# Four stage borders of a hybrid decoder step on one Trainium2 core: a head norm reordered, new queries built earlier, value rows written by panel, two mixture tiles and one third of a panel done before a border

## The chip, the core and the metric

The kernel runs on one core of a Trainium2 chip. The metric is the device time of one execution in microseconds. Engines are called by the names of the profile: PE (TensorE, with PEld for its weight loads), DVE (VectorE), ACT (ScalarE), POOL (GpSimd) and SP (SyncE, whose queue issues nearly every DMA here).

## What is computed

One inference step of a two-layer decoder trunk, for a prompt of 1024 tokens and 8 samples of 4 new tokens each (1056 token columns in all). Cut to what matters:

```
for l in range(2):
    h = rmsnorm(x, g_norm1[l]) * (1 + sc1) + sh1            # sh, sc, g come from c @ w_ada
    q_a, k_a, v_a, i, f, o, u, q_c, k_c, v_c, f_c = split(h @ w_in[l] + b_in[l])
    ha = sigmoid(o) * headnorm(mlstm(q_a, k_a, v_a, i, f))   # chunks of 128, 4 heads
    hb = pool_mix(u)                                         # windows 2, 4, 8, 16
    hc = forgetting_attention(q_c, k_c, v_c, f_c)            # 6 heads of 64; samples read 16 pages of cache each
    x = x + g1 * (concat(ha, hb, hc) @ w_out[l])
    h2 = rmsnorm(x, g_norm2[l]) * (1 + sc2) + sh2
    x = x + g2 * (relu(h2 @ w_up[l])**2 @ w_down[l])
y = rmsnorm(x, g_final)
```

Keys, values, forget values and the recurrent states of both layers are outputs too.

## The kernel before

Everything is feature major: 128 features on the partitions, 1056 token columns along the free axis. Large products are done in two-part fp32r: an operand is a high part (a cast) and a low part (operand minus high part), and each product is three matmuls, high x high, low x high and high x low. The 1056 columns are cut in three *parts* of 352 (`CW`), so one panel of 128 output features is three *thirds* of 24 matmuls each (`part_product`, L307; in the projection `third`, L851). Weights come in panels of 128 x 1024: SP loads one into `raw`, POOL casts it to `whi` (L295), DVE subtracts to `wlo` (L300).

A layer is three blocks of code, and between two blocks all engines meet at a barrier; between the layers there are two barriers, since one more block clears semaphores. All orders are written out by hand, per engine, with semaphore waits.

- **`projection(l)`**: 21 panels (rows of `F`, in the order `PANEL_ROWS`). From panel 9 on, chunk `u` of the mLSTM is interleaved with the thirds of panel `n = START + u`; chunk 8 (`CH`) is the samples. DVE works through `square_heads(u-1)`, `clip(u)`, `keys(u)` (L1281, L1288), `scale_query(u)` (L1299 to L1306), `norm_heads(u-1)` (L1365 to L1367), `weigh(u)`, `join(u-1)`. PE turns the normed heads with `turn_heads` (L967), which waits for `norm_heads`. The last thing on PE is `turn_values` (L979), which turns the value rows into `vC`. In layer 1 the block begins with panels 0 and 1 part by part, because the norm of the last 352 columns is unfinished: `sums` (L593), a third of panel 0 with `spread` (L604) inside it, and so on.
- **`attention(l)`**: 24 units (3 pairs of heads x 8 query blocks) of the prompt, with the 8 samples interleaved, one per three units: `scores(b)` (L1712) needs 16 pages of the cache, four per *step*, and `past_mixed(b)` (L1748) uses them. Pages lie in a ring of 24 buffers `KVp`, six steps. SP's program there is serial: pages of the first sample, three rows of past sums (L1567), 8 page numbers (each a register load), 8 pages, 16 page numbers, and then per step a wait for the ring and four pages. The start of the block also has GpSimd's `row_spread` (L1596), masks, `Qb` (the new queries of the samples, laid out in blocks, L1610); PE's `forget` (L1646), whose results DVE and ACT copy into `Fb` (L1831, L1965). `Fb` overwrites value rows of `F`, so these copies wait until the value rows are stored in `o_v` (L782).
- **`out_and_mlp(l)`**: the output projection by phases: thirds (panel, part) in the order (0,0), (1,0), (0,1), (1,1), (2,0), (2,1), ... Its operand is the mixture, eight tiles of `F` (`MIX`), cast to `hH` (ACT L2257 for part 0, POOL L2100 for parts 1 and 2) and reduced to `hL` by DVE (L2300). `x` was spilled and is reloaded (L2073). Then the MLP, and at its end, again by phases, residual and norm for the next layer.

PE's third waits read, for instance, as

```
def turn_heads(u):
    pe.wait_ge(S["normal"], u + 1)
...
by_phases(0, (hH, hL), lambda part, k: pe.wait_ge(mixed, KT * part + k + 1))
```

## Time and profile before

| | |
|---|---|
| runs shown | 2780.46, 2784.61, 2788.09 us (median 2784.61) |
| profiled execution, its own time | 2787.31 us |
| its span | 2785.5 us |
| PE busy | 2691.4 us (97%) |
| DVE, ACT, POOL busy | 1238.0, 633.8, 264.4 us |
| mean granted clock | 0.988 |
| projection of layer 0, attention, output projection and MLP | about 54 to 381 us, 381 to 557, 557 to 1431 |
| the same of layer 1 | 1431 to 1750, 1750 to 1928, 1928 to 2785 |

The profile is one execution recorded by the hardware. PE is busy nearly throughout, so what matters is the short list of places where it is not: the view of waits gives, per engine and line, who was waited for, in total, how often, and the longest. A timeline shows start, duration, engine, line, operation, and in square brackets the idle time just before with its releaser; matmuls overlap, so durations of single matmuls are longer than their distance. The view by windows gives busy times of a stretch and the granted clock of PE, where 1.00 is 2.4 GHz and 0.50 is 1.2 GHz.

### The profile page before, as it was taken

Reading aid. Unit: us, or ns where it says so; the run is one execution under the profiler, and the core shown is the slowest. Engines: PE = TensorE matmul, PEld = TensorE weight load, DVE = VectorE, ACT = ScalarE, POOL = GpSimd, SP = SyncE. Lnnn points to the kernel's source line nnn. Section 1 sums busy time; section 2 is a strip of 40 time slices with the busy share of each in tenths; the row PEclk is TensorE's granted clock in tenths of the full one; section 3 lists DMA queues with packets and bytes.
Section 4 is the critical chain, followed back from the end, with each engine's and each line's share of the span. In section 5 each row is a group of like instructions: output and inputs, shape, how many; then the busy total and the mean of one; then the engine's idle time right before and its main releaser. Section 6 shows DMA issues by size and latency. Waiting matters only on the chain. (4 is left out here: it accounts for less than half of the span.)

```text
span 2785.5 us, 48553 instructions
## 1 busy us (share of the span) xinstructions
PE 2691.4 (97%) x20596; PEld 2511.2 (90%) x20596; DVE 1238.0 (44%) x2223; ACT 633.8 (23%) x1044; POOL 264.4 (9%) x342
## 2 busy tenths in 40 slices
PE   5999989999999999999999999898999999999998
PEld 4999966699999999999989999566999999999998
DVE  5735535647423423324457354456563242242344
ACT  4334334423110110001133432343221000000012
POOL 0101100020000000001111010001100000000010
PEclk9999999999999999999999999999999999999999
DMA  8440168631222221111133102885212111111111
GB/s 308 155 109 31 67 243 319 246 116 46 84 84 91 76 91 61 54 46 46 61 112 118 52 31 88 316 324 197 81 54 71 46 45 53 46 54 46 46 55 69
DMA packets 106873, 295.37 MB, mean 106 GB/s; under 512 B 19605, under 2 KB 32790, under 8 KB 104610
## 3 DMA queue, kind: packets, MB, share of 16 engines
q1 hardware_dynamic: 106498, 291.49, 30.3%
q8 instruction: 163, 2.67, 0.4%
q0 software_dynamic: 160, 0.79, 0.1%
q14 instruction: 52, 0.43, 0.0%
HBM read 269.61 MB, written 22.63 MB: 105 GB/s over the span
## 5 line engine op out<-in xcount | busy, mean ns | idle before, releaser
L307 PE MATMUL PS<-hH,whi 128*128 128x352 f32 x1632 | 534.3, 327 | 8.0 <-DVE hL L2300 6.4
L307 PE MATMUL PS<-hL,whi 128*128 128x352 f32 x1632 | 525.4, 322 | 0.0
L307 PE MATMUL PS<-hH,wlo 128*128 128x352 f32 x1632 | 524.9, 322 | 0.0
L307 PE MATMUL PS<-aH,whi 128*128 128x352 f32 x1344 | 439.4, 327 | 4.0 <-PEq L384 3.2
L307 PE MATMUL PS<-aL,whi 128*128 128x352 f32 x1344 | 432.2, 322 | 0.0
L307 PE MATMUL PS<-aH,wlo 128*128 128x352 f32 x1344 | 431.9, 321 | 0.0
L295 POOL CAST whi<-raw 128x1024 fp32r<-128x1024 f32 x158 | 166.5, 1054 | 1673.2 <-PE PS L307 1332.6
L307 PEld LDWEIGHTS PS<-hH,whi 128*128 128x128 f32 x1632 | 307.8, 189 | 16.1 <-issue 12.7
L307 PEld LDWEIGHTS PS<-hL,whi 128*128 128x128 f32 x1632 | 308.5, 189 | 0.0
L307 PEld LDWEIGHTS PS<-hH,wlo 128*128 128x128 f32 x1632 | 307.8, 189 | 0.0
L851 PE MATMUL PS<-aH,whi 128*128 128x352 f32 x912 | 303.6, 333 | 1.9 <-ACT F L1060 1.9
L851 PE MATMUL PS<-aH,wlo 128*128 128x352 f32 x912 | 293.6, 322 | 0.0
L851 PE MATMUL PS<-aL,whi 128*128 128x352 f32 x912 | 293.2, 322 | 0.0
L307 PEld LDWEIGHTS PS<-aH,whi 128*128 128x128 f32 x1344 | 253.5, 189 | 9.5 <-issue 4.7
L307 PEld LDWEIGHTS PS<-aL,whi 128*128 128x128 f32 x1344 | 253.9, 189 | 0.0
L307 PEld LDWEIGHTS PS<-aH,wlo 128*128 128x128 f32 x1344 | 253.1, 188 | 0.0
L300 DVE TENSOR_TENSOR wlo<-raw,whi 128x1024 fp32r<-128x1024 f32 x160 | 195.8, 1223 | 126.3 <-POOL whi L295 124.6
L2384 DVE TENSOR_TENSOR aH<-ev 128x1056 fp32r<-128x1056 f32 x64 | 84.0, 1313 | 272.1 <-ACT ev L2269 272.1
L2269 ACT ACTIVATE ev<-PS 128x1056 f32<-128x1056 f32 x64 | 67.6, 1056 | 573.2 <-PE PS L307 573.2
L851 PEld LDWEIGHTS PS<-aH,whi 128*128 128x128 f32 x912 | 171.7, 188 | 10.5 <-issue 4.2
L851 PEld LDWEIGHTS PS<-aL,whi 128*128 128x128 f32 x912 | 172.2, 189 | 0.4
L851 PEld LDWEIGHTS PS<-aH,wlo 128*128 128x128 f32 x912 | 171.9, 189 | 0.0
(367 smaller groups left out, 3563.2 us busy)
## 6 DMA issues: line engine op xcount, KB each, us to landing
KVp<-kv SPq DMA_DIRECT2D x256, 384.0 KB, 7.3
raw<-w_ff SPq DMA_DIRECT2D x128, 512.0 KB, 3.6
raw<-w_in SPq DMA_DIRECT2D x42, 512.0 KB, 3.5
wad_single<-w_ada SPq DMA_DIRECT2D x40, 512.0 KB, 3.6
wad<-w_ada SPq DMA_DIRECT2D x32, 512.0 KB, 5.6
x_spill<-x SPq DMA_DIRECT2D x2, 4224.0 KB, 13.3
wada<-w_first SPq DMA_DIRECT2D x8, 1024.0 KB, 7.0
raw<-w_out SPq DMA_DIRECT2D x16, 512.0 KB, 4.1
```

The source lines that it names most:

```text
L295: nc.gpsimd.tensor_copy(home(n)[0][:], raw[spot(n)][:]).then_inc(s["high"], 1)
L300: nc.vector.tensor_tensor(wl[:], raw[spot(n)][:], wh[:].bitcast(F32), ALU.subtract).then_inc(s["split"], 1)
L307: last = nc.tensor.matmul(PS[:, 3 * p + part, 0:CW], w[:, k, :], a[:, k, part * CW:(part + 1) * CW], start=k == 0 and w is wh and a is hig ...
L851: last = nc.tensor.matmul(PS[:, part, 0:CW], w[:, k, :], a[:, k, part * CW:(part + 1) * CW], start=k == 0 and w is whi[n % 2] and a is aH, ...
L2269: nc.scalar.activation(three(ev[n % 2][:]), banks(n % 2), ACT.Relu).then_inc(s["room"], NCH)
L2384: link(nc.vector.tensor_tensor(aH[:, j, :], t, t, ALU.mult))
```

## The change

It edits five places.

1. **Projection, unit 8.** DVE does `norm_heads(7)` ahead of `keys(8)` and `scale_query(8)`; PE does `turn_heads(8)` one third later.
2. **Value rows.** `o_v` is written by three DMAs, one per row, the first two ahead of the sixth page, the third after it. Three cache pages (7th to 9th) are no longer issued in the projection but at the start of the attention. The waits for `o_v` follow: `Fb` needs rows 0 and 1, two of the `PT` buffers need row 2.
3. **New queries.** GpSimd's `row_spread`, masks, `Qb` and `cum` are made at the end of its projection block. ACT begins the attention with a one-element Exp.
4. **Mixture.** Tiles 0 and 1 of part 0 are cast (POOL) and reduced (DVE) during units 18 to 22 of the attention; part 1 is cast by ACT instead of POOL; DVE splits weight panel 1 after all eight tiles of part 0 instead of after four; SP loads weight panel 2 ahead of `x`; POOL splits panel 2 first.
5. **Layer border.** The 24 matmuls of (panel 0, part 0) of layer 1's projection are done at the end of layer 0's last block, ahead of both barriers.

```diff
 projection, SP:
+                def values_rows(j):
+                    sp.wait_ge(s["room"], NCH * (NPAN - 2 + j))
+                    sp.dma_start(o_v[bass.ds(l, 1), :, j].rearrange("a p n -> (a p) n"), F[:, VC + j, :]).then_inc(value_rows[j], 16)
+                values_rows(0)
+                values_rows(1)
                 sp.wait_ge(s["done"], NCH * NPAN)
                 page_in(sp, l, len(early), first_numbers[len(early)])
-                sp.wait_ge(s["room"], NCH * NPAN)
-                sp.dma_start(o_v[bass.ds(l, 1)].rearrange("a p b n -> (a p) b n"), F[:, VC:VC + 3, :]).then_inc(row_store, 16)
-                for n in range(len(early) + 1, 2 * GP + 1):
-                    page_in(sp, l, n, first_numbers[n])
+                values_rows(2)
 projection, POOL, at the end:
+                pool.wait_ge(S["update"], CH + 1)
+                pool.wait_ge(s["room"], NCH * (ORDER.index(QC + 2) + 1))
+                pool.wait_ge(row_store, 48)
+                pool.wait_ge(rows_done, 1)
+                new_queries(pool)
 projection, PE:
                     sums(pe, 1)
+                    pe.sem_inc(s["done"], 1)
                     for part in range(NCH):
...
-                        for n in range(2):
+                        for n in range(0 if part else 1, 2):
...
+                    third(n, 1)
                     if u == CH + 3:
                         turn_heads(CH)
-                    third(n, 1)
 projection, DVE:
                     if u <= CH:
                         clip(u)
+                    if u == CH:
+                        norm_heads(u - 1)
+                    if u <= CH:
                         keys(u)
                         scale_query(u)
-                    if 1 <= u <= CH:
+                    if 1 <= u < CH:
                         norm_heads(u - 1)
 attention, SP:
-                for n in range(2 * GP + 1, PAGES):
+                for n in range(len(early) + 1, PAGES):
                     page_in(sp, l, n, first_numbers[n])
 attention, POOL (the calls that new_queries now makes are gone from its start):
+                    if i in (2 * CH + 2, 2 * CH + 4):
+                        pool.wait_ge(S["low"], 4 * CH)
+                        k = (i - 2 * CH) // 2 - 1
+                        nc.gpsimd.tensor_copy(mix_tile(hH, k), mix_tile(F, MIX[k])).then_inc(mix_high, 1)
 attention, DVE and ACT, for Fb, and for the PT buffers 4 and 5:
-                            dve.wait_ge(values_out, 64)
+                            dve.wait_ge(values_out, 80)
+                            if at_ in (4, 5):
+                                eng.wait_ge(values_out, 80)
+                                eng.wait_ge(last_values_out, 64)
 attention, DVE:
+                    if i in (2 * CH + 4, 2 * CH + 6):
+                        k = (i - 2 * CH) // 2 - 2
+                        dve.wait_ge(mix_high, k + 1)
+                        nc.vector.tensor_tensor(mix_tile(hL, k), mix_tile(F, MIX[k]), mix_tile(hH, k).bitcast(F32), ALU.subtract).then_inc(mix_low, 1)
 attention, ACT, first:
+                nc.scalar.activation(share[0:1, 0:1], c("eps", 1), ACT.Exp)
 out_and_mlp, SP:
-                load_x(0)
                 for n in range(2, AHEAD):
...
                     load(sp, n)
+                    if n == 2:
+                        load_x(0)
 out_and_mlp, POOL:
-                for part in range(1, NCH):
-                    for k in range(KT):
-                        mix_high(part, k)
-                    split_high(pool, part + 1)
-                for n in range(4, KT):
+                split_high(pool, 2)
+                for k in range(KT):
+                    mix_high(2, k)
+                for n in range(3, KT):
                     split_high(pool, n)
 out_and_mlp, PE, after the last panels:
+                        else:
+                            pe.wait_ge(s["split"], NP + 1)
+                            for k in range(KT):
+                                pe.wait_ge(N["low"], 2 * KT + k + 1)
+                                part_product(0, 0, k, aH, aL)
 out_and_mlp, ACT:
-                for k in range(KT):
-                    nc.scalar.activation(hH[:, k, cut(0)], F[:, MIX[k], cut(0)], ACT.Copy).then_inc(high, 1)
+                for part in range(2):
+                    for k in range(0 if part else MIXED_EARLY, KT):
+                        nc.scalar.activation(hH[:, k, cut(part)], F[:, MIX[k], cut(part)], ACT.Copy).then_inc(high, 1)
 out_and_mlp, DVE:
-                for k in range(KT):
+                for k in range(MIXED_EARLY, KT):
                     mix_low(0, k)
-                    if k == 3:
-                        split_low(dve, 1)
+                split_low(dve, 1)
                 for k in range(KT):
                     mix_low(1, k)
```

How the instructions stand at three places. First SP at the border from projection to attention (the branches are the end of one block and the start of the next; an ISA row is the address of the page that follows), before:

```order
L1499 DMA KVp_569<-kv 128x768
L782 DMA o_v<-F 128x3168
L1499 ISA
L1499 DMA KVp_570<-kv 128x768
L1499 ISA
L1499 DMA KVp_571<-kv 128x768
L1499 ISA
L1499 DMA KVp_572<-kv 128x768
L735 UNCONDITIONAL_BRANCH
L1563 UNCONDITIONAL_BRANCH
L1499 ISA
L1499 DMA KVp_573<-kv 128x768
```

and SP there after the change:

```order
L782 DMA o_v<-F 128x1056 x2
L1512 ISA
L1512 DMA KVp_569<-kv 128x768
L782 DMA o_v<-F 128x1056
L736 UNCONDITIONAL_BRANCH
L1599 UNCONDITIONAL_BRANCH
L1512 ISA
L1512 DMA KVp_570<-kv 128x768
L1512 ISA
L1512 DMA KVp_571<-kv 128x768
L1512 ISA
L1512 DMA KVp_572<-kv 128x768
```

Three pages moved behind the barrier: the attention's SP program now begins with ten pages instead of seven.

Second, DVE in the projection at unit 8, before:

```order
L1270 TENSOR_SCALAR E_519<-PS,cols 32x32 x4
L1281 TENSOR_SCALAR wKs<-PS,cols 32x64 x4
L1288 TENSOR_TENSOR wKb<-wKs,con 32x2048
L1299 TENSOR_TENSOR qss<-F,PS 128x64
L1301 COPY alast<-PS 128x8 x2
L1306 COPY qB<-qss 64x8x4 x4
L1365 RECIPROCAL small<-small 128x4
L1366 TENSOR_TENSOR small<-small 128x4
L1367 TENSOR_TENSOR heads<-num_539,small 128x384
```

and after the change:

```order
L1279 TENSOR_SCALAR E_519<-PS,cols 32x32 x4
L1374 RECIPROCAL small<-small 128x4
L1375 TENSOR_TENSOR small<-small 128x4
L1376 TENSOR_TENSOR heads<-num_539,small 128x384
L1290 TENSOR_SCALAR wKs<-PS,cols 32x64 x4
L1297 TENSOR_TENSOR wKb<-wKs,con 32x2048
L1308 TENSOR_TENSOR qss<-F,PS 128x64
```

The three instructions that end in `heads` moved ahead of the five groups of keys and queries.

Third, DVE at the border from attention to output projection, before:

```order
L1960 TENSOR_TENSOR wlo_67<-raw_63,whi_65 128x1024
L1925 COPY F<-PS 128x3x32
L1562 UNCONDITIONAL_BRANCH
L2278 UNCONDITIONAL_BRANCH
L2300 TENSOR_TENSOR hL<-F,hH 128x352 x4
L300 TENSOR_TENSOR wlo_68<-raw_64,whi_66 128x1024
L2300 TENSOR_TENSOR hL<-F,hH 128x352 x12
```

and after the change:

```order
L1993 TENSOR_TENSOR wlo_67<-raw_63,whi_65 128x1024
L1954 COPY F<-PS 128x3x32
L1598 UNCONDITIONAL_BRANCH
L2318 UNCONDITIONAL_BRANCH
L2340 TENSOR_TENSOR hL<-F,hH 128x352 x6
L300 TENSOR_TENSOR wlo_68<-raw_64,whi_66 128x1024
L2340 TENSOR_TENSOR hL<-F,hH 128x352 x8
```

Two of the sixteen subtractions are gone from the block, and the split of weight panel 1 stands behind six of them instead of four.

## Rows read from the trace of the kernel before

**Rows 1.** Waits of PE, whole span: for whom, total us, times, longest.

```profile
PE PS L1712 <- DMA KVp<-kv: 9.9, 8, 3.2
PE PS L307 <- DVE hL L2300: 6.4, 4, 2.7
...
PE PS L967 <- DVE heads L1367: 3.7, 2, 1.9
...
PE PS L1696 <- DVE Fb L1831: 2.9, 1, 2.9
PE PS L1646 <- POOL row_spread L1596: 2.8, 2, 1.4
...
PE PS L967 <- DVE headss L1367: 2.4, 2, 1.2
...
PE PS L1696 <- POOL Qb L1610: 1.8, 1, 1.8
```

**Rows 2.** Windows: us, busy PE, PEld, DVE, ACT, POOL, granted clock, DMA share, GB/s.

```profile
330.50:334.50 4.00, 4.00 (x17) 4.00 (x16) 0.52 (x3) 0.00 (x0) 0.00 (x0) 0.57 0.00 0
...
559.50:566.50 7.00, 6.29 (x21) 5.73 (x22) 7.00 (x12) 2.48 (x5) 3.67 (x5) 0.51 1.03 403
1430.00:1437.00 7.00, 5.74 (x34) 5.50 (x34) 1.06 (x2) 0.33 (x1) 0.98 (x1) 0.52 0.81 327
...
1928.00:1935.50 7.50, 5.84 (x20) 5.41 (x21) 7.05 (x11) 4.61 (x10) 5.80 (x8) 0.54 0.79 294
```

**Rows 3.** The same view, layer 1, behind the same wait for heads.

```profile
1699.00:1703.00 4.00, 2.87 (x19) 2.87 (x20) 2.38 (x10) 0.00 (x0) 0.00 (x0) 1.00 0.02 4
```

**Rows 4.** Timeline of layer 0, unit 8: ACT's root, DVE's norm of the heads.

```profile
322.77 0.30 ACT L1070 ACTIVATE small<-small,con 128x4 f32<-128x4 f32 x1 [3.29 <-DVE small L1357]
...
328.96 0.56 DVE L1367 TENSOR_TENSOR heads<-num,small 128x384 f32<-128x384 f32 x1
```

**Rows 5.** Timeline of SP in the attention of layer 0: pages.

```profile
381.49 3.92 SPq L1499 DMA_DIRECT2D KVp<-kv  x7
...
405.23 4.13 SPq L1499 DMA_DIRECT2D KVp<-kv  x8
```

**Rows 6.** Timeline of PE there: scores of the first and the second sample.

```profile
395.27 0.86 PE L1712 MATMUL PS<-KVp,Qb 128*32 128x128 f32 x24 [0.91 <-DMA KVp<-kv]
...
417.39 1.51 PE L1712 MATMUL PS<-KVp,Qb 128*32 128x128 f32 x24 [3.04 <-DMA KVp<-kv]
```

**Rows 7.** Window ahead of the second batch of pages.

```profile
403.00:406.00 3.00, 3.00 (x28) 2.23 (x26) 2.42 (x4) 1.16 (x3) 0.00 (x0) 1.00 0.08 30
```

**Rows 8.** Timeline of DVE in the attention, ahead of units 21 and 23.

```profile
531.00 1.09 DVE L1842 CUSTOM_DVE_ANT_0 Trow<-Fb,PS 128x896 f32<-128x896 f32 x1 [1.17 <-PE PS L1662]
...
542.61 0.82 DVE L1842 CUSTOM_DVE_ANT_0 Trow<-Fb,PS 128x640 f32<-128x640 f32 x1 [1.00 <-PE PS L1662]
```

**Rows 9.** Timeline of layer 0, start of the output projection.

```profile
557.82 2.89 DVE L2300 TENSOR_TENSOR hL<-F,hH 128x352 fp32r<-128x352 f32 x4 [1.05 <-ACT hH L2257]
558.71 0.40 PE L307 MATMUL PS<-hH,whi 128*128 128x352 f32 x1 [2.68 <-DVE hL L2300]
...
560.63 1.49 DVE L300 TENSOR_TENSOR wlo<-raw,whi 128x1024 fp32r<-128x1024 f32 x1
...
562.04 5.86 DVE L2300 TENSOR_TENSOR hL<-F,hH 128x352 fp32r<-128x352 f32 x12
...
578.25 0.43 PE L307 MATMUL PS<-hH,ohi 128*128 128x352 f32 x1
```

**Rows 10.** The chain that ended last: start, us; one third of a panel.

```profile
2066.35 3.92 PE PS L307 x24
```

**Rows 11.** Timeline of the border between the layers.

```profile
1429.41 0.95 DVE L633 SCALAR_TENSOR_TENSOR aL<-end_wide,mod,aH 128x704 fp32r<-128x704 f32 x1
...
1431.26 0.52 PE L593 MATMUL PS<-end_sums,con 128*32 128x88 f32 x8 [3.93 <-DVEq L1379]
...
1458.45 0.81 PE L1021 MATMUL PS<-con 128*128 128x384 f32 x2
```

More of the change, by code:

```diff
@@ L714, in projection @@
         cached, cacheable = sem("in_values_moved"), sem("in_values_turned")
+        value_rows = (row_store, row_store, pool_store)
         sam = lambda t, r=HA: t[0:r, SEQ:TOK].rearrange("p (b t) -> p b t", b=NB)
@@ L1015, in _ @@
                                 last = part_product(n, part, k, aH, aL)
-                                if part == 0 and n == 0 and k == 5:
+                                if part == 0 and k == 5:
                                     spread(pe, 1)
@@ L1443, in trunk @@
     MIX = (OA, OA + 1, OA + 2, U, U + 1, QC, QC + 1, QC + 2)
+    MIXED_EARLY = 2
     PAIRS, QW = HC // 2, PAST // 4 + NT
@@ L1538, in trunk, with pair_rows, new_queries @@
     piece_user = [u for u, e, a in piece]
+    def pair_rows(j):
+        nc.gpsimd.tensor_copy(row_spread[:], c("head", 32 + HC)[:, 2 * j * P:(2 * j + 2) * P]).then_inc(sem("fox_rows"), 1)
+    def new_queries(pool):
+        masks, zero, cumulated, query = (sem(f"fox_{n}") for n in ("masks", "zero", "cumulated", "query"))
+        pair_rows(0)
+        nc.gpsimd.tensor_copy(one_hot[:], ident).then_inc(masks, 1)
+        nc.gpsimd.tensor_copy(future[:], c("tri")).then_inc(masks, 1)
+        nc.gpsimd.memset(Qb[:], 0.0).then_inc(zero, 1)
+        nc.gpsimd.tensor_copy(cum[:], LC[0:HC, SEQ:TOK].rearrange("p (b t) -> p b t", b=NB)).then_inc(cumulated, 1)
+        pool.wait_ge(zero, 1)
+        for j in range(3):
+            pool.wait_ge(cumulated, j + 1)
+            nc.gpsimd.tensor_tensor(cum[:, :, j + 1], cum[:, :, j], cum[:, :, j + 1], ALU.add).then_inc(cumulated, 1)
+            for e in range(2):
+                r = slice(64 * e, 64 * e + 64)
+                h = 2 * j + e
+                nc.gpsimd.tensor_copy(Qb[r, :, j, h * NT:(h + 1) * NT], F[r, QC + j, SEQ:TOK].rearrange("p (b t) -> p b t", b=NB)).then_inc(query, 1)
     def attention(l):
@@ L1544, in attention @@
         S = {n: sem(f"fox_{n}") for n in names}
-        values_out = sem("in_rows_out")
+        values_out, last_values_out = sem("in_rows_out"), sem("in_pool_out")
         out_loaded, out_high, out_split = [sem(f"ff_loaded{n}") for n in range(2)], sem("ff_high"), sem("ff_split")
+        mix_high, mix_low = sem("out_mix_high"), sem("out_mix_split")
+        mix_tile = lambda t, k: t[:, k, 0:CW]
         lfl = [sem(f"fox_sums{i}") for i in range(3)]
@@ L1595, in spread_rows @@
                             is_full(pool, ("forget", j - 1, e, 1))
-                    nc.gpsimd.tensor_copy(row_spread[:], c("head", 32 + HC)[:, 2 * j * P:(2 * j + 2) * P]).then_inc(S["rows"], 1)
-                spread_rows(0)
-                nc.gpsimd.tensor_copy(one_hot[:], ident).then_inc(S["masks"], 1)
-                nc.gpsimd.tensor_copy(future[:], c("tri")).then_inc(S["masks"], 1)
-                nc.gpsimd.memset(Qb[:], 0.0).then_inc(S["zero"], 1)
-                nc.gpsimd.tensor_copy(cum[:], LC[0:HC, SEQ:TOK].rearrange("p (b t) -> p b t", b=NB)).then_inc(S["cumulated"], 1)
-                pool.wait_ge(S["zero"], 1)
-                for j in range(3):
-                    pool.wait_ge(S["cumulated"], j + 1)
-                    nc.gpsimd.tensor_tensor(cum[:, :, j + 1], cum[:, :, j], cum[:, :, j + 1], ALU.add).then_inc(S["cumulated"], 1)
-                    for e in range(2):
-                        r = hp(e)
-                        h = 2 * j + e
-                        nc.gpsimd.tensor_copy(Qb[r, :, j, h * NT:(h + 1) * NT], F[r, QC + j, SEQ:TOK].rearrange("p (b t) -> p b t", b=NB))\
-                            .then_inc(S["query"], 1)
+                    pair_rows(j)
                 pool.wait_ge(S["query"], 6)
@@ L1971, in forget @@
                         if j == 0 and half == 0:
-                            act.wait_ge(values_out, 64)
+                            act.wait_ge(values_out, 80)
                         if j and half == 0:
@@ L2295, in mix_low @@
                 def mix_low(part, k):
-                    if part:
-                        dve.wait_ge(late_high, KT * (part - 1) + k + 1)
+                    if part == 2:
+                        dve.wait_ge(late_high, k + 1)
                     else:
-                        dve.wait_ge(high, k + 1)
+                        dve.wait_ge(high, KT * part + k + 1)
                     nc.vector.tensor_tensor(hL[:, k, cut(part)], F[:, MIX[k], cut(part)], hH[:, k, cut(part)].bitcast(F32), ALU.subtract).then_inc(mixed, 1)
```

## The prediction

> **What bounds the kernel now.** I read the table of busy times first (PE 97%), then the waits of PE, then the granted clock by windows, and last the timelines of the borders. PE sets the time, so the change is worth what it takes out of PE's idle time and out of its slow stretches. The waits [rows 1] name what it aims at: the heads of chunk 7 (3.7 us in two layers), the heads of the samples (2.4), the first mixture tiles (6.4), and at the start of the attention `row_spread` (2.8), the new queries (1.8) and `Fb` (2.9). Behind some of these waits PE's granted clock stands at the lower of its two levels, 1.2 GHz instead of 2.4 [rows 2]: 0.57 over 4 us behind the heads of layer 0, 0.51 to 0.54 over 7 us at both output projections and at the border of the layers. In layer 1 the same wait for heads left it at 1.00 [rows 3]. A third of a panel is 24 matmuls in 3.92 us [rows 10], 0.163 each. One more wait stands in the list: pages of the cache, 9.9 us [rows 1].
>
> The profiled execution took 2787.3 us, which is 2.7 above the median of the runs shown (2784.6). I sum against 2787.3 and take the 2.7 off at the end. A measurement of this kernel can tell about 0.3%, 8.4 us, from no change.
>
> **Heads of chunk 7.** The root is there at 323.1, the norm is done only at 329.5, behind keys and queries [rows 4]. Moved ahead, it is done some 5 us earlier, before PE asks. Its longest wait, 1.9, goes in both layers: -3.7. The slow stretch behind it in layer 0 costs 4 x 0.43 = 1.7 and goes too: -5.4. What DVE does later by the 0.9 us of the three instructions (keys, queries) is asked for two panels on, and `qB` waits for GpSimd anyway.
>
> **Heads of the samples.** One third, 3.92 us, now covers a wait of 1.2: -2.4 in two layers. The join has the last third as cover.
>
> **Queries, rows of values, pages.** At the start of the attention PE's three waits (2.8 + 1.8 + 2.9 = 7.5 in two layers) go away, but I book nothing for them. PE then reaches `scores(0)` earlier, and its last step starts when the last of 16 pages lands, at 395.3 [rows 6], where PE waited 0.9 already. The bytes ahead of that page are the same as before, so it lands within a microsecond of that time. Then comes `scores(1)`: its last step started at 417.39, after a wait of 3.04 for pages [rows 6], and those pages are issued from 405.23 on [rows 5]. From 403 to 406 the DMA engines had almost nothing to do (share 0.08) [rows 7], so it was SP's serial program that set this time: seven pages, three rows of sums, 8 numbers, 8 pages, 16 numbers. The change puts three more pages at its head, 3.92 / 7 = 0.56 us each [rows 5]: everything behind is 1.7 later, and PE, which waits at this place in both layers, with it: **+3.4**. The bounds: it cannot cost more than 3.75 per layer, the time by which the first moved page is issued later; it can gain, at best, the 0.9 to 2 per layer by which the first pages could come earlier.
>
> Here a rule speaks against the change. The Trainium skill, "DMA: Bandwidth & Descriptors", Rules for kernel authors, says to issue a DMA early, compute, and wait late; three pages are issued later. By the rule alone the cost is that full 3.75 per layer, 7.5 in place of 3.4; it is the third rival.
>
> **Mixture tiles in the attention.** DVE gets two subtractions of 0.49 (12 in 5.86 [rows 9]), behind the reciprocals of units 20 and 22. It sits idle for 1.17 and 1.00 just there [rows 8]: nothing. If the cover were gone, they would cost 1.0 per layer; that end stays for the range.
>
> **Start of the output projection.** PE stopped at 558.71 - 2.68 = 556.0 and began panel 2 at 578.25 [rows 9]: 22.2 us for four thirds, 15.7. After the change PE may start when the barrier lets go; DVE's first subtraction began at 557.8 behind one cast of ACT, so that is about 557.3. Six matmuls on tiles 0 and 1: 558.3. Tile 2 is ready at 558.3, and each further one 0.5 later (GpSimd, beside which four took 2.89, has no part 1 to cast): tile 7 at 560.9, its matmuls done at 561.4. Then the split of panel 1, 1.49 (row 560.63), ends at 562.4: a new wait of 1.0 takes the place of the old one at tile 4. Three thirds more, 11.8: 574.2. That is 4.0 earlier, twice: **-8.0**. It supposes the clock stays up: 1.3 us idle is less than what preceded the slow stretches, 2.7 here, and the waits of 1.2 at the samples' heads left it up. If it does not, 2.2 of the 4.0 are lost again. Next late would be the split of panel 2, which hangs on the residual and arrives within 0.2 us of need.
>
> **Border of the layers.** PE stopped at 1427.3 and stood 3.93 until DVE's last low part (1430.36) and two barriers (0.9) were through [rows 11]. Now it works 3.9 us there. Seven eighths of its operand are ready, the last at 1430.4, so it ends at 1431.2; the barriers add 0.9. Of the idle time 3.0 goes. The clock, 0.52 over 7 us [rows 2], stays up: of the 3.4 that it lost, 0.6 fell into the idle time; the small matmuls of the sums gain little from a faster clock, so I take 2.0 of the other 2.8. **-5.0.** The norm's chain for the last part has one third, 3.9, less of cover. Behind the spread PE still has 54 matmuls (8.8) before it asks for the first tile and 3.4 more before the last, so I book nothing; it is what comes late next (rival 4). Panel 2 then starts near 1453.5 instead of 1458.45.
>
> **Sum.** -5.4 - 2.4 + 3.4 - 8.0 - 5.0 = -17.4: 2769.9 against its own execution, 2767.2 against the median. I say **2768**.
>
> **The rivals.**
> 1. *The clock stays low at both output projections.* For: it fell there in both layers. Against: the shorter gap. +4.4, about 2772.
> 2. *The pages do not hold the attention.* SP's 1.7 is hidden, and the first pages land up to 2 earlier. -3.4 and up to -3: 2762. Against it: the idle DMA engines of rows 7.
> 3. *The moved pages cost their full delay.* +4.1: 2772. Against: the pages are issued 0.56 apart, and what SP does behind them is only three pages longer.
> 4. *The waits go, others take their place.* Splits of panels 1 and 2 late in the output projection, the norm's tail late at the layer border, the moved subtractions in the way: over 9 us in sum, within 0.3%, about 2778.
> 5. *Slower.* At the start of the attention PE waits for pages longer than before, from about 387 to 394 and again up to 419, and its clock falls and stays low. What the other borders gain is 20.8; to be slower by 8.4, each layer must lose 14.6, and since half speed costs half of a stretch, the clock would have to stay low for about 30 us of each attention. The longest stretches in rows 2 are 7. About 2795.
> 6. *It doesn't do what it says*: if DVE's norm were still late because the root waits, heads would keep their 3.7; the root is 6 us early [rows 4], so no.
>
> **How the numbers follow.** The forecast (2764 to 2771) 0.50, rival 1 0.17, rival 2 0.13, rival 3 0.07, rival 4 0.10, rival 5 0.03. Faster by over 0.3% (under 2776.3): the first four, 0.87. Within: 0.10. Slower: 0.03. The range of 8 in 10 reaches to rivals 1 to 3 and takes in the scatter of the runs, 4 us either way of their median: 2760 to 2777.
>
> **What would show it.** Right: no wait for heads in the list of PE's waits; a clock of 1.00 behind them; the wait for pages grown from 9.9 to over 14, its longest near 5 to 6; the second batch of pages issued 24.6 to 25.4 us behind the attention's first page instead of 23.7; panel 2 of the output projection 18 us behind the attention's last matmul; the wait between the layers 0.9 to 1.0. Wrong: waits for pages at or below 9.9 (rival 2), a clock near 0.5 behind 557 (rival 1), new waits for `wlo`, `olo` or the norm's low parts over 1 us (rival 4).

## The result and the profile after

Runs of the changed kernel took 2771.36 us (median of 7, 2767.75 to 2775.78), and those of the kernel before on the same chips 2786.16: a ratio of 0.9946, 95% interval 0.9936 to 0.9956, so 15.0 us less (12.3 to 17.8). The prediction was 2768, which is 16.6 less than the median that it started from.

The profiled execution of the kernel after took 2775.77 us, 4.4 above its own median, at a granted clock of 0.990 (before 0.988). Its span is 2774.1 us, 11.4 less than before. Its waits of PE, as in [rows 1] (for whom, total us, times, longest):

```profile
PE PS L1738 <- DMA KVp<-kv: 21.7, 12, 4.0
...
PE PS L307 <- PEq L1598: 2.9, 2, 1.4
PE PS L1672 <- PEq L736: 2.2, 2, 1.3
...
PE PS L307 <- DVE olo L300: 1.3, 2, 0.9
...
PE PS L593 <- DVEq L1388: 0.9, 1, 0.9
PE PS L1722 <- DVE Fb L1860: 0.8, 1, 0.8
```

The waits for both kinds of heads, `row_spread` and `Qb` are gone, `Fb` fell from 2.9 to 0.8, the mixture from 6.4 to 2.9, the layer border from 3.9 to 0.9. The wait for pages grew from 9.9 to 21.7. PEq stands for PE's sequencer, here at a barrier.

To see where the time went I cut both profiles at four instructions of PE that every version has: the first transpose of the values (TV) and the last matmul of the attention, in each layer. In us:

| stretch | before | after | difference |
|---|---|---|---|
| start to TV of layer 0 | 377.2 | 373.0 | -4.2 |
| both attentions, TV to their last matmul | 359.3 | 367.7 | **+8.4** |
| end of the attention of layer 0 to TV of layer 1 | 1190.1 | 1177.8 | -12.3 |
| end of the attention of layer 1 to the end | 858.8 | 855.5 | -3.3 |
| sum | 2785.5 | 2774.1 | -11.4 |

Three stretches gave 19.8 and the attentions took 8.4 back. What they took back is idle time but for 1.1 us: the view by windows over the two attentions gives lengths, then PE's busy time with its count. Before, and after:

```profile
sum 359.29, PE 327.39 PEld 220.08 DVE 193.63 ACT 145.77 POOL 17.93; mean PE 163.70 PEld 110.04 DVE 96.81 ACT 72.89 POOL 8.96
```

```profile
sum 367.73, PE 328.45 PEld 217.87 DVE 195.57 ACT 145.71 POOL 12.91; mean PE 164.22 PEld 108.93 DVE 97.78 ACT 72.86 POOL 6.46
```

PE did 327.4 and 328.5 us of work; it idled 31.9 before and 39.3 after. In layer 0 the timeline of PE shows where, in the rows that answer to [rows 6]:

```profile
388.03 0.86 PE L1738 MATMUL PS<-KVp,Qb 128*32 128x128 f32 x24 [4.04 <-DMA KVp<-kv]
391.83 1.51 PE L1738 MATMUL PS<-KVp,Qb 128*32 128x128 f32 x24 [2.94 <-DMA KVp<-kv]
...
413.69 0.86 PE L1738 MATMUL PS<-KVp,Qb 128*32 128x128 f32 x24 [2.02 <-DMA KVp<-kv]
417.59 1.51 PE L1738 MATMUL PS<-KVp,Qb 128*32 128x128 f32 x24 [3.04 <-DMA KVp<-kv]
```

The last step of `scores(0)` comes 18.8 us behind TV (TV is at 373.02; before it was 18.0 behind 377.24), that of `scores(1)` 44.6 behind it, before 40.2. SP's queue, to be held against [rows 5]:

```profile
377.11 7.14 SPq L1512 DMA_DIRECT2D KVp<-kv  x10
384.31 2.15 SPq L1603 DMA_DIRECT2D LFb<-past_sums  x3
391.05 5.15 SPq L1512 DMA_DIRECT2D KVp<-kv  x8
...
405.21 9.18 SPq L1512 DMA_DIRECT2D KVp<-kv  x16
```

Ten pages took 7.14, 0.71 each instead of 0.56, and the next eight 5.15. Before, those eight took 3.97:

```profile
392.25 3.97 SPq L1499 DMA_DIRECT2D KVp<-kv  x8
```

So the second batch is issued 28.1 us behind the first page, before 23.7. In layer 1 the ten took 6.20 and it is 26.3.

The borders, by windows (us, busy times, granted clock, DMA share, GB/s), as in [rows 2]:

```profile
354.50:358.50 4.00, 4.00 (x19) 3.94 (x16) 3.70 (x16) 0.00 (x0) 3.32 (x14) 0.57 0.02 4
389.00:399.50 10.50, 6.80 (x49) 3.42 (x53) 2.56 (x11) 1.94 (x5) 0.63 (x3) 0.51 0.97 347
...
559.50:566.50 7.00, 7.00 (x35) 7.00 (x35) 6.84 (x15) 6.64 (x16) 3.48 (x1) 0.76 0.91 325
1430.00:1437.00 7.00, 6.50 (x55) 5.84 (x56) 2.74 (x6) 1.39 (x3) 0.98 (x1) 1.00 0.85 344
...
1920.00:1927.00 7.00, 6.86 (x41) 6.55 (x42) 6.64 (x14) 6.85 (x16) 2.63 (x1) 1.00 0.79 276
```

Behind the layer border and at the second output projection the clock stayed at 1.00. At the first it was low for half of the stretch. At 354.5 there is a slow stretch where there was none. The slow stretch of the attention, behind the waits for pages, now lasts some ten microseconds; it isn't new, since before the change the attention of layer 0 had two of about seven:

```profile
385.00:392.00 7.00, 6.71 (x60) 4.07 (x60) 1.49 (x8) 2.48 (x6) 0.75 (x4) 0.53 1.03 405
416.00:423.00 7.00, 5.61 (x50) 4.83 (x52) 1.97 (x5) 1.69 (x4) 0.31 (x2) 0.51 1.01 395
```

The windows also tell what the DMA engines did. The first row below lies in the wait of `scores(0)`, the second just ahead of the batch at 405.21, where [rows 7] had 0.08:

```profile
385.00:389.00 4.00, 0.86 (x24) 0.59 (x24) 0.00 (x0) 1.26 (x4) 0.00 (x0) 1.00 0.98 363
402.00:405.00 3.00, 3.00 (x28) 2.34 (x28) 2.53 (x5) 1.27 (x3) 0.00 (x0) 1.00 0.01 3
```

While the first sixteen pages were on their way the DMA engines were full (0.91 to 0.99 in each four microseconds from 377 to 401); behind them they stood idle.

### The profile page after: what moved, and what is told of

The parts are those of the page before. It is cut to its first block and busy times, and to the rows that moved or that the text cites. A ratio compares the mean times of both kernels' runs of the same rounds, so it can differ in the third digit from the quotient of the medians.

```text
span 2774.1 us, 48567 instructions
## 1 busy us (share of the span) xinstructions
PE 2687.3 (97%) x20596; PEld 2505.8 (90%) x20596; DVE 1233.3 (44%) x2223; ACT 638.2 (23%) x1058; POOL 262.3 (9%) x330
```

## The experiments

Theory **S**: what set the end of the attention's first 45 us is SP's serial program (reads of page numbers, issues of pages), and the longer it is behind the barrier, the longer PE waits. Rival **D**: the transfers themselves, or the stores of the value rows in front of them. All ratios are to the kernel before on the same chip; 0.001 is 2.8 us.

### One part of the change at a time

Each kernel is the kernel before with one part of the diff; of each part a line or two stands here. One instruction changed its part: the one-element Exp with which ACT begins the attention is in the kernels "output projection alone" and "without the start of the attention", and not in "start of the attention alone".

**Start of the attention alone** (queries, rows of values, three pages).

```diff
+                values_rows(2)
-                for n in range(len(early) + 1, 2 * GP + 1):
-                    page_in(sp, l, n, first_numbers[n])
...
+                new_queries(pool)
```

> The kernel before (2786.2) with only the part for the start of the attention: new queries laid out by GpSimd in the projection, rows of values stored by panel, three pages moved behind the barrier. In the profile of the whole change the attention grew by 6.0 and 2.4 us over the two layers (179.3 on the mean to 183.9). Theory S (ten pages instead of seven start behind the barrier, SP's serial program ends that much later, and PE waits for pages longer than it waited for the queries): this part alone is slower, 2790 to 2795; waits for row_spread, Qb and Fb gone (7.5 us to under 1.5), waits for pages 19 to 23 us. Rival A (this part is worth nothing either way, and the mixture tiles lengthened the attention): 2784 to 2788.

Measured: ratio 1.0019 (1.0010 to 1.0029), **+5.3 us**. The two attentions measured 368.4, 9.1 more than before; the wait for pages 19.6. This was theory S's result, and it puts rival A aside: the mixture tiles aren't in this kernel. Of the 9.1, only 3.7 is idle time (35.6 instead of 31.9); PE's busy time grew by 5.4, with the granted clock of layer 0 at 0.94 instead of 0.96. Layer 0:

```profile
390.69 0.86 PE L1729 MATMUL PS<-KVp,Qb 128*32 128x128 f32 x24 [1.64 <-DMA KVp<-kv]
394.82 1.51 PE L1729 MATMUL PS<-KVp,Qb 128*32 128x128 f32 x24 [3.27 <-DMA KVp<-kv]
...
416.50 0.86 PE L1729 MATMUL PS<-KVp,Qb 128*32 128x128 f32 x24 [0.65 <-DMA KVp<-kv]
420.43 0.86 PE L1729 MATMUL PS<-KVp,Qb 128*32 128x128 f32 x24 [3.07 <-DMA KVp<-kv]
```

The missing Exp shows on ACT. In this kernel the table load stands behind the copies of `Fb`, in the kernel after ahead of them:

```profile
382.31 1.28 ACT L2000 ACT_TABLE_LOAD   x1
```

```profile
376.98 1.28 ACT L2029 ACT_TABLE_LOAD   x1 [0.28 <-PEq L736]
```

The first exponential then comes 7.1 us behind TV instead of 6.3. What this is worth isn't shown, since no run has this part with the Exp.

**Heads alone.**

```diff
+                    if u == CH:
+                        norm_heads(u - 1)
+                    if u <= CH:
                         keys(u)
...
+                    third(n, 1)
                     if u == CH + 3:
                         turn_heads(CH)
-                    third(n, 1)
```

> The kernel before (2786.2) with only the order of the heads changed: norm of the last chunk ahead of the new keys on DVE, and the samples' heads one third later on PE. The prediction's terms are -5.4 and -2.4: 2778 to 2779. Theory W (a wait is worth its idle time, and the slow stretch of the clock behind it goes elsewhere): only the waits go, 3.7 and 2.4, so -6: 2780. Rival: the part is worth under 3, because other waits for DVE take the place.

Measured: 0.9990 (0.9981 to 0.9999), **-2.8 us**. That is the rival's size, but not its reason: no other wait for DVE took the place. The interval's other end, -5.3, is near theory W. No wait for heads is left in its profile; the stretches before TV are 2.9 and 2.7 shorter, for 3.0 of waits each. But its attentions measured 361.9, 2.6 more, with 11.4 of waits for pages instead of 9.9; of the 2.6, 2.0 is busy time of PE, most of it in layer 0, where the granted clock was 0.95 instead of 0.96.

**Layer border alone.**

```diff
+                        else:
+                            pe.wait_ge(s["split"], NP + 1)
+                            for k in range(KT):
+                                pe.wait_ge(N["low"], 2 * KT + k + 1)
+                                part_product(0, 0, k, aH, aL)
```

> The kernel before (2786.2) with only one third of the next layer's first panel worked ahead of the border. The prediction's term is -5.0 (idle 3.0, clock 2.0): 2781. By the profile of the whole change, which showed no slow stretch at the border, 3.1 idle and 3.4 clock: as low as 2780. Theory W: the slow stretch turns up at another place: 2783.

Measured: 0.9985 (0.9976 to 0.9994), **-4.2 us**. By the ratio the time is 2782, between the forecasts of the prediction and of theory W. The stretch that holds the border is 6.4 shorter, and behind the border, which is at 1431.4 here, the clock stays up:

```profile
1431.00:1438.00 7.00, 6.49 (x55) 5.82 (x56) 2.71 (x6) 1.39 (x3) 0.98 (x1) 1.00 0.91 373
```

This holds in every profile: from 1420 to 1450 the granted clock was 1.00 in all nine kernels with this part and 0.89 to 0.94 in all five without it.

**Output projection alone.**

```diff
+                    if i in (2 * CH + 4, 2 * CH + 6):
...
+                for part in range(2):
+                    for k in range(0 if part else MIXED_EARLY, KT):
```

> The kernel before (2786.2) with only the output projection's start changed: two mixture tiles split in the attention, ACT casting the first two parts, the load of x one place later. The prediction's term is -8.0; the whole change showed -3.2 and -3.8 from the attention's last matmul to panel 2: 2778 to 2780. Rival A (the two tiles lengthen the attention through DVE and GpSimd, by up to 2 per layer): 2780 to 2783, and the attention measures 181 or more on the mean instead of 179.6.

Measured: 0.9981 (0.9972 to 0.9990), **-5.3 us**, 2781.3, a time that rival A had forecast. From the end of an attention on, the stretches are 3.9 and 3.4 shorter, and the clock stayed at 1.00 at both output projections. The attentions measured 179.2 and 181.7, 180.4 on the mean: rival A's 181 isn't reached, but half a microsecond per layer can't be told from scatter.

The three gains sum to -12.3. The next run has them together.

**The change without the start of the attention.**

> The changed kernel (ratio to before 0.9946, -15) with the part for the start of the attention taken back: queries, rows of values and pages as before; heads, border and output projection as changed. Alone that part cost +5.3 (interval 2.7 to 8.1). If the parts add up, this is the faster kernel: -20, 2766. The other three alone gave -2.8, -4.2 and -5.3, which sum to -12.3: if that sum holds, 2773.5, and the part for the attention is worth something only beside the others. Rival: the attention measures 359 to 361 us over two layers, as before (after the change 367.7), and the time is 2764 to 2768.

Measured: 0.9941 (0.9928 to 0.9955), **-16.4 us**, 2768.87. The attentions:

```profile
sum 360.66, PE 328.86 PEld 220.70 DVE 195.93 ACT 146.07 POOL 19.63; mean PE 164.43 PEld 110.35 DVE 97.96 ACT 73.04 POOL 9.81
```

Idle 31.8, as before the change. So the attention part, which removes three waits (7.5 us), brings nothing that can be measured: it cost 5.3 alone (without its Exp), and with the others the two kernels can't be told apart (0.9941 against 0.9946, intervals overlapping). Both forecasts of the time, 2766 and 2773.5, lie at the ends of the interval, so this run doesn't decide whether the parts add up.

### What holds the pages

**Three pages issued ahead of the barrier again.**

```diff
                 values_rows(2)
+                for n in range(len(early) + 1, 2 * GP + 1):
+                    page_in(sp, l, n, first_numbers[n])
```

> The changed kernel (median 2771.4) with three pages of the cache (n = 6, 7, 8) issued in the projection again, behind the last row of values. Theory S (SP's serial program behind the barrier sets the time of the second batch of pages): from the first page behind the barrier to the first page of the second batch it takes 24 to 26 us instead of 28.1 and 26.3, the waits of scores(1) shrink by 1.7 to 3.7 per layer, the list's wait for pages falls from 21.7 to 14 to 18, the time is 2765 to 2768. Rival D (the stores of the values, now three DMAs close to the pages, slow the transfers): waits for pages stay above 20 and the time within 2 us of 2771.4. Rival C (the scatter of the granted clock made the attention longer, not the pages): the time stays too, but the waits shrink.

Measured: 0.9944 (0.9931 to 0.9957), 2771.9: no difference, as rival D had said, against theory S's forecast of 2765 to 2768. The second batch did come 25.1 us behind the first page behind the barrier in both layers, as theory S had said, and the wait for pages fell, to 12.8. But it fell at `scores(0)`; the waits of `scores(1)` didn't shrink (5.9 and 5.5, after the change 5.1 and 2.1). In place of the others:

```profile
PE PS L1674 <- PEq L736: 6.5, 2, 3.7
```

The barrier at the attention's start waits for SP, which is issuing these pages: 6.5 us instead of 2.2. So on either side of the barrier PE waits for what SP has still to issue: counted from TV, the second batch came at 31.2 and 32.0, after the change at 32.2 and 30.9.

**One store of the value rows.**

```diff
-                values_rows(0)
-                values_rows(1)
...
-                values_rows(2)
+                sp.wait_ge(s["room"], NCH * NPAN)
+                sp.dma_start(o_v[bass.ds(l, 1)].rearrange("a p b n -> (a p) b n"), F[:, VC:VC + 3, :]).then_inc(row_store, 16)
```

> The changed kernel (2771.4) with the three rows of values stored by one DMA behind the sixth page, as before the change; the three pages stay behind the barrier. Theory S: nothing but the place of 1.6 MB moves, the time is within 2 us of 2771.4, the wait for pages 20 to 23, the second batch still 26 to 28 us behind the first page. Rival D: the first sixteen pages land earlier, the waits of scores(0) (7.0 in layer 0, 4.8 in layer 1) fall by 2 or more per layer, and the time is 2765 to 2768.

(The waits for `o_v` are those of the kernel before.) Measured: 0.9956 (0.9943 to 0.9969), 2773.5, a little over theory S's "within 2 us" and not D's gain. But the waits at `scores(0)` fell, to 1.5 and 0.9, as D had said, the wait for pages to 15.1 (theory S: 20 to 23), and `Fb` took their place:

```profile
PE PS L1734 <- DMA KVp<-kv: 15.1, 8, 3.4
PE PS L1718 <- DVE Fb L1855: 5.4, 2, 3.3
```

`Fb` waits for the stored rows. The last step of `scores(0)` came 19.1 and 18.7 us behind TV, after the change 18.8 and 19.6: nearly the same place.

**Numbers read four by four.** All reads behind the first sixteen pages stand just before the four pages they belong to.

```diff
-                numbers = {n: page_number(sp, n) for i in range(STEPS, RING) for n in pages_of(i)}
...
-                    if (i - RING) % STEPS == 0:
-                        numbers = {n: page_number(sp, n) for m in range(i, min(i + STEPS, NB * STEPS)) for n in pages_of(m)}
+                    numbers = {n: page_number(sp, n) for n in pages_of(i)}
```

> The changed kernel (2771.4) in which SP reads the numbers of each four pages just before it issues them, instead of 8 before the second eight pages and 16 before each later batch. The count of reads and of DMAs is the same. Theory S: the first page of step 6 is issued when step 0 of the first past mixture is done (about 399.5 in layer 0 instead of 405.2) and step 7 about 3.6 us earlier than now; the waits of scores(1) (5.1 us in layer 0, 2.1 in layer 1) go, the wait for pages falls from 21.7 to 13 to 16, and the time is 2763 to 2766. Rival D (transfers, not SP, hold the pages): the waits of scores(1) stay within 1 us and the time within 2 us of 2771.4.

Measured: 0.9937 (0.9924 to 0.9950), 2768.3; not told apart from 0.9946, and short of theory S's 2763 to 2766. The waits of `scores(1)` are gone but for 0.3, so they did hang on SP's order. Others came: 0.95 at TV+63, 1.1 at TV+143, 2.1 at TV+163 in layer 1. The wait for pages is 19.3, not 13 to 16.

**The same edit in the kernel before.**

> The kernel before (2786.2) with the same edit, numbers of four pages read just before their DMAs. Theory S: its wait of scores(1) for pages (3.0 us in layer 0, as much in layer 1) goes, since its second batch too was issued behind 16 reads while the DMA engines stood idle: 2779 to 2782. Rival D: within 2 us of 2786.2.

Measured: 0.9986 (0.9977 to 0.9995), 2783.2, -3.9, a little short of theory S. Both waits of 3.0 and 3.2 at `scores(1)` are gone, yet the attentions measure 359.2, as before (359.3), since late waits came:

```profile
1902.57 0.86 PE L1710 MATMUL PS<-KVp,Qb 128*32 128x128 f32 x24 [1.70 <-DMA KVp<-kv]
```

The attentions gave nothing in this execution; where the 3.9 of the medians come from, I can't say.

**Four by four for the first ten steps only.**

```diff
-                    if (i - RING) % STEPS == 0:
+                    if i < RING + STEPS or (i - RING) % STEPS == 0:
+                        ahead = 1 if i < RING + STEPS else STEPS
```

> The changed kernel (0.9946) in which SP reads the page numbers four by four for the first ten steps only, and sixteen at a time, ahead of the wait, behind them. Reading four by four everywhere removed the waits of scores(1) but brought others late in the attention (2.1, 1.1 and 1.0 us in layer 1). Theory S, refined (SP's own work, 16 reads of 0.57 and 16 pages of 0.56 a batch, 18 of some 20 us, holds the pages; the order of reads decides which batch pays): scores(1) without waits and none over 0.7 behind TV+60, the attention 362 to 364 us over two layers, 2765 to 2768. Rival D (the DMA engines' throughput holds them): waits for pages stay at 18 or more, 2769 to 2772.

Measured: 0.9957 (0.9943 to 0.9971), median 2773.6: no gain, and neither forecast of the time met (the wait for pages was 13.6). Its profiled execution, 2767.2, happens to be its fastest, and still shows what went wrong: `scores(1)` starts without a wait, `scores(2)`, 20 us later, has the wait instead, at TV+62 (and 3.0 in layer 1):

```profile
408.24 2.83 PE L1738 MATMUL PS<-KVp,Qb 128*32 128x128 f32 x96
...
433.06 0.86 PE L1738 MATMUL PS<-KVp,Qb 128*32 128x128 f32 x24 [2.42 <-DMA KVp<-kv]
```

By these two runs a changed order of the reads chose which sample waits, and gave nothing that the medians show.

**And two value rows stored before the early pages.**

```diff
+                values_rows(0)
+                values_rows(1)
                 for n, page in enumerate([page_number(sp, n) for n in range(len(early))]):
                     page_in(sp, l, n, page)
                 first_numbers.update({n: page_number(sp, n) for n in range(len(early), PAGES)})
-                values_rows(0)
-                values_rows(1)
```

> e5_first_numbers with the first two rows of values stored before the early pages instead of behind the eleven reads (they were issued at 371.3, 1.7 us before the transposes of the values, though their panels were done at 349 and 361). Theory D2 (in the first 15 us of the attention the DMA engines are the limit, and 1 MB of stores stands in front of the pages): scores(0)'s waits (7.0 and 4.8 us) fall by 2 or more in each layer, 2761 to 2764. Rival (SP's ten issues behind the barrier hold scores(0)): those waits stay within 1 us, the time is that of e5_first_numbers.

Measured: 0.9955 (0.9941 to 0.9968), 2774.2, a miss for D2. The pages are issued later:

```profile
361.05 1.38 SPq L779 DMA_DIRECT2D o_v<-F  x2
367.43 9.04 SPq L1512 DMA_DIRECT2D KVp<-kv  x6
```

The early pages start 6.3 us before TV, in the kernel after 10.3 (362.71 against 373.02). Waits at `scores(0)` were 3.7 and 6.0, and 3.4 and 3.0 without this edit. Since the edit delays SP's pages as well as advancing the stores, it doesn't test D2 by itself.

**No reads at all behind the first sixteen pages.** This is the run that separates SP from the transfers.

```diff
-                numbers = {n: page_number(sp, n) for i in range(STEPS, RING) for n in pages_of(i)}
+                numbers = {n: n % kv.shape[1] for i in range(STEPS, RING) for n in pages_of(i)}
```

(and the same for the later batches). This kernel leaves out following the table: it reads other pages, in order, so the outputs for the samples are others.

> The changed kernel (ratio to before 0.9946, -15) in which SP reads no page numbers behind the first sixteen pages of a layer: page n of the cache is taken instead of the page that the table names, so the table is not followed there and the bytes and the DMAs stay as they are. 224 reads of 0.57 us leave SP. Theory S (SP's reads and issues together hold the pages of the second to fourth request): the waits at scores(1) (TV+40 to TV+45) go and none of over 1 us takes their place at scores(2) (TV+60 to TV+65); the waits at scores(0), which stand behind the ten pages after the barrier and have no read ahead of them, stay within 1.5 us of 7.0 and 4.8; the attention measures 356 to 361 us over two layers instead of 367.7 and the ratio is 0.991 to 0.993. Rival D (the transfers themselves hold scores(1) too): its waits stay above 2 us, ratio 0.994 to 0.996. TV is the first transpose of the values.

Measured: 0.9920 (0.9905 to 0.9934), 2763.2, **7 us less than the change** (whose interval, 0.9936 to 0.9956, it doesn't touch), in the middle of theory S's 0.991 to 0.993. The attentions, at the lower end of its range:

```profile
sum 355.75, PE 328.98 PEld 219.28 DVE 195.74 ACT 145.72 POOL 12.91; mean PE 164.49 PEld 109.64 DVE 97.87 ACT 72.86 POOL 6.46
```

Idle 26.8 instead of 39.3. `scores(1)` and `scores(2)` run through, and what is left is `scores(0)`:

```profile
386.12 0.86 PE L1738 MATMUL PS<-KVp,Qb 128*32 128x128 f32 x24 [0.93 <-DMA KVp<-kv]
390.00 0.86 PE L1738 MATMUL PS<-KVp,Qb 128*32 128x128 f32 x24 [3.01 <-DMA KVp<-kv]
...
408.33 2.83 PE L1738 MATMUL PS<-KVp,Qb 128*32 128x128 f32 x96
...
428.55 2.83 PE L1738 MATMUL PS<-KVp,Qb 128*32 128x128 f32 x96
```

The bytes and the number of DMAs are the same, so D falls for the second and later samples, which agrees with the DMA engines' share of 0.01 ahead of the second batch. (That pages in order come faster than pages by the table was not tested by itself.) The waits at `scores(0)` are 3.9 in layer 0, outside the 5.5 to 8.5 expected, and 4.9 in layer 1. Its ten pages took 6.63 to issue, in the kernel after 7.14; part of the 7.0 there was that one execution. Whether these waits come from SP's ten issues or from the transfers, which keep the DMA engines full up to there (1.01 to 1.02 in this kernel from 379 to 395), no run separates: for `scores(0)` rival D stays open.

The size fits. Between the eight pages that SP issued from 391.05 to 396.20 and the batch at 405.21 stand 16 reads, 0.56 each. A sample costs SP 16 reads (9.0 us), 16 pages (9.2, the row at 405.21) and one row of sums (0.7): 18.9. `scores(1)` and `scores(2)` of this last kernel, which waits for neither, are 20.2 apart (408.33 and 428.55). SP had 1.3 us of slack per sample. By this sum a later start, whether from the barrier, a store or a stalled issue, is caught up by only 1.3 us per sample, and the waits for pages are how PE sees it.

## Why the prediction was right, and where it wasn't

| term | predicted | measured, in the profiles | alone, in the medians |
|---|---|---|---|
| heads of chunk 7 and of the samples | -7.8 | -6.7: start to TV -4.0 (mean of nine kernels with this part against five without, 372.6 and 376.6), layer 1 -2.7 (heads alone) | -2.8 |
| output projections | -8.0 | -7.0 (22.2 to 19.0 and 22.1 to 18.3, end of the attention to panel 2) | -5.3 |
| layer border | -5.0 | -5.5 (31.1 to 25.6), -6.4 in its stretch when done alone | -4.2 |
| start of the attention | +3.4 | +8.4 | +5.3 |
| what no term covers | 0 | -0.6 | |
| sum | -17.4 | -11.4 | -7.0 |

Together, the medians gave -15.0.

**Heads.** The step held. The norm ends at 323.45 and PE asks at 326.65:

```profile
322.89 0.56 DVE L1376 TENSOR_TENSOR heads<-num,small 128x384 f32<-128x384 f32 x1
...
326.65 0.49 PE L975 MATMUL PS<-con,heads 128*128 128x128 f32 x3
```

Both waits went in both layers. The clock behind them is the soft part: the slow stretch at 330.5 is gone, and one at 354.5 came, with no wait in front of it. The 1.7 that the prediction put on the clock was a property of the execution: with the same wait for heads in place, the kernel of the layer border alone and that of the attention's start alone show 1.00 there (see the last section). And of what is won before TV the attention may return a part (2.6 when done alone).

**Output projection.** The mechanism held; the size was off by 1.0. The first matmul starts 1.4 after the attention's last (predicted 1.3), DVE's split of `wlo` ends at 563.5 instead of 562.4, and PE waits for `olo` once in each layer, 0.39 and 0.93, which I had within 0.2 of need. The clock fell for 3.5 us at the first and not at the second: rival 1 came true in half.

```profile
559.66 2.70 DVE L2340 TENSOR_TENSOR hL<-F,hH 128x352 fp32r<-128x352 f32 x6 [1.05 <-ACT hH L2297]
562.28 1.22 DVE L300 TENSOR_TENSOR wlo<-raw,whi 128x1024 fp32r<-128x1024 f32 x1
```

```profile
576.86 0.43 PE L307 MATMUL PS<-hH,ohi 128*128 128x352 f32 x1 [0.39 <-DVE olo L300]
```

The two moved subtractions stand in DVE's idle time, at 531.15 and 542.93, and cost nothing that can be seen, as booked.

**Layer border.** The wait is 0.88 (predicted 0.9 to 1.0) and nothing came late behind it:

```profile
1430.37 0.36 PE L593 MATMUL PS<-end_sums,con 128*32 128x88 f32 x8 [0.88 <-DVEq L1388]
...
1451.24 0.81 PE L1030 MATMUL PS<-con 128*128 128x384 f32 x2
```

**Start of the attention.** This is the term that was mis-sized, in the step "three more pages at its head, 0.56 us each: everything behind is 1.7 later". The direction was right, and so was "I book nothing" for the three waits that go. The last step of `scores(0)`, which I had within a microsecond, came 0.8 and 1.6 later, counted from TV. Wrong was the price of an issue. The ten pages were issued at 0.71 each and the eight behind the sums took 1.2 more than before, so the second batch was 4.2 later against TV in layer 0 (32.2 instead of 28.0) and 2.5 in layer 1. The sign I had named, the second batch 24.6 to 25.4 us behind the first page, measured 28.1 and 26.3. What SP stalls on in a DMA issue the trace doesn't say; it was not isolated. The dear issues fall where the DMA engines' share was 0.91 to 0.99, but so do the cheap ones of the kernel before (0.98 from 381 to 385). The delay, 3.4 on the mean, is nearly the 3.75 of rival 3. The execution with +8.4 stood 4.4 above its median. The difference of the medians less the other stretches, -15.0 less -19.6, would leave +4.6 for the term, an estimate that mixes medians with single profiles. Alone it cost 5.3, and taking it back out of the whole change gave only 1.4.

I also took this for a loss of one place, 1.7 at the second sample. It is a loss that the order of SP's work can only move: with the reads gone the attentions of the profiles are 12 us shorter, and the medians 7. In that light the wait of 3.04 at `scores(1)` that was there before the change [rows 6] was the first sign of an engine with 18.9 of 20.2 us of work.

The time itself, 2771.4 against 2768, is inside the range. Not all of that is the sum's merit. By the medians of the parts, the three gains were 12.3 of the 20.8 forecast and the loss 5.3 instead of 3.4; their sum, -7.0, would have been 2779, beyond the range's end at 2777. Why the whole gave -15.0 was not settled, so that it landed 3.4 from the forecast may in part be luck.

Did it pay to change the attention's start? The runs can't show that it did. Without it the kernel takes 2768.9 and with it 2771.4, in intervals that overlap. None of the variants that keep the computation (0.9937 to 0.9957) can be told from the change.

## What to carry to other kernels

- Before removing waits at the start of a stage, ask what its next operand's supplier is doing. Here PE's waits for queries and `Fb` overlapped the arrival of the pages; removed, they turned into waits for pages.
- Add up the serial work of a queue engine per iteration (reads of registers and issues) and hold it against the iteration's length. At 18.9 of 20.2 us it is nearly the bound, though the engine shows no busy time in the profile. Here the reads were half of it. The Trainium skill, "DMA: Bandwidth & Descriptors", Rules for kernel authors, says that spreading DMAs over several issuing engines gives no bandwidth and only saves the sequencer's issue time; by these runs SP's time, for reads and issues, is what was short here, but spreading was not tried.
- Judge an edit of 0.2% by ratios over rounds and cut the profiles at common instructions. The longest stretch away from the attention repeated within 0.8 us for all eight kernels with the same parts (1177.6 to 1178.4), while the attentions of kernels whose medians can't be told apart ranged from 361 to 369.

## What was not expected of the hardware

- **A slow stretch of the clock isn't tied to the wait before it.** The five kernels that keep the order of the heads all have the same wait, PE busy for 2.1 of the 4 us from 326.5. Behind it the granted clock was 0.57 before the change, 0.66 in the output projection alone, and 1.00 in the other three. The start of the attention alone:

```profile
326.50:330.50 4.00, 2.16 (x15) 1.87 (x14) 2.99 (x13) 0.64 (x1) 1.98 (x2) 1.00 0.00 0
330.50:334.50 4.00, 4.00 (x27) 4.00 (x27) 1.18 (x5) 0.00 (x0) 0.00 (x0) 1.00 0.02 6
```

  And the slow stretch at 354.5, in which PE was busy all the time, doesn't come from moving the heads. It is also in the layer border alone, whose heads are unchanged, and not in the change without the start of the attention (1.00 from 350 to 368), whose heads are changed. What stands right in front of it, in the kernel after and in the layer border alone, is 4.7 us of 136 small matmuls of the samples, the last 64 of them 32 partitions high. The kernel after, and the layer border alone:

```profile
351.75 2.89 PE L962 MATMUL PS<-vAs,wKb 32*64 32x97 f32 x64
```

```profile
357.50:361.00 3.50, 3.50 (x15) 3.50 (x14) 3.28 (x15) 0.00 (x0) 0.00 (x0) 0.53 0.00 0
```

  The change without the start of the attention runs the same small matmuls and goes on at 1.00, so these alone don't decide it either. With the heads alone, and with numbers read four by four, a slow stretch began at 550.5, 4.5 us before the attention's end. The mean went from 0.988 to 0.990, which over 2780 us is some 6 us at full speed, but executions of the changed kernel alone lay between 0.988 and 0.992. A wait removed should be booked at its idle time, and the clock's part as an uncertain extra, unless several profiles agree, as they do at the layer border.
- **SP's issue of one page has no fixed price.** Seven took 3.92 us in the kernel before [rows 5], 0.56 each; after the change ten took 7.14 in layer 0 and 6.20 in layer 1; without reads the first eight behind the sums took 4.28; with three pages ahead of the barrier the ten took 7.73.
- **The parts don't add up well.** Singly they gave -2.8, -4.2, -5.3 and +5.3, in sum -7.0; together -15.0. The intervals of the four and of the whole, each about 2.5 either way, allow for some 6 of the 8 between them. A part of the rest may be the Exp, which the attention's part lacked when it was alone; whether there is an interaction besides, with PE and SP meeting at the attention's start in another order each time, was not settled.
